# The dilated layer as one rolling sequence: four heads at a time, pair steps between the next heads' products

## The reference, cut to what matters

```
for g, (window, dil) in enumerate(DIL_PAIRS):
    qg, kg = rope(q[g]), rope(k[g])
    o_g, lse_g = banded attention of qg, kg, v[g], every dil-th token
wts = softmax(lse over the groups)
branch = sum of wts[g] * o_g
mem_out = memory_attention(qm, mk, mv)
y = concatenate(branch, mem_out) * silu(gate)
h = layer_norm(ALPHA * h + y @ w_out)
```

## Time and profile before

| | us |
|---|---|
| median of 3 runs | 1480.76 |
| lowest, highest | 1479.58, 1488.71 |
| the profiled execution | 1486.72 |
| its span | 1484.9 |
| busy TensorE, VectorE, ScalarE, GpSimd | 1354.7, 875.3, 655.5, 67.2 |
| the dilated layer's products, first to last | 327.5 to 695.7 |

### The profile page before, as it was taken

The page is one execution under the profiler, slowest core; times in us unless marked ns, Lnnn a source line. Parts: engine busy times, 40 slices in busy tenths (PEclk is TensorE's granted clock), DMA queues, the critical chain, the costliest instruction groups (busy, mean ns, idle before and its releaser), DMA issues. The chain is left out here.

```text
span 1484.9 us, 19718 instructions
## 1 busy us (share of the span) xinstructions
PE 1354.7 (91%) x7972; PEld 1167.0 (79%) x7972; DVE 875.3 (59%) x1455; ACT 655.5 (44%) x905; POOL 67.2 (5%) x48
## 2 busy tenths in 40 slices
PE   6998988989997899988999868999999878999997
PEld 6887885668886678876887857799988867799996
DVE  6546594667843387445535587565456587565454
ACT  4523425434344444552432537354443446344432
POOL 0000000000004400150000000000000000000000
PEclk9998998999999999998999889999999988999999
DMA  9405530145552045423304333355654332355661
GB/s 301 143 29 170 170 114 29 32 139 170 173 196 86 29 149 189 144 86 120 113 30 132 124 99 114 94 176 184 200 181 150 124 121 85 114 175 177 188 200 70
DMA packets 134240, 197.52 MB, mean 133 GB/s; under 512 B 4332, under 2 KB 77318, under 8 KB 134022
## 3 DMA queue, kind: packets, MB, share of 16 engines
q1 hardware_dynamic: 134022, 196.22, 40.7%
q0 software_dynamic: 128, 0.04, 0.0%
HBM read 195.20 MB, written 1.05 MB: 132 GB/s over the span
## 5 line engine op out<-in xcount | busy, mean ns | idle before, releaser
L1209 ACT ACTIVATE w_hi<-w_raw 128x2048 fp32r<-128x2048 f32 (+5 forms) x190 | 346.8, 1828 | 628.0 <-PE bank L432 595.9
L1554 DVE TENSOR_TENSOR w_lo<-w_raw,w_hi 128x2048 fp32r<-128x2048 f32 (+5 forms) x190 | 414.0, 2185 | 209.6 <-ACT w_hi L1209 200.2
L430 PE MATMUL bank<-h_hi,w_hi 128*128 128x256 f32 x976 | 281.9, 289 | 11.4 <-DVE w_lo L1554 7.9
L431 PE MATMUL bank<-h_lo,w_hi 128*128 128x256 f32 x976 | 279.3, 286 | 0.0
L432 PE MATMUL bank<-h_hi,w_lo 128*128 128x256 f32 x976 | 279.1, 286 | 0.0
L430 PE MATMUL bank<-w_hi,r_hi 128*128 128x512 f32 (+3 forms) x536 | 207.1, 386 | 9.7 <-DVE w_lo L1554 7.0
L431 PE MATMUL bank<-w_lo,r_hi 128*128 128x512 f32 (+3 forms) x536 | 205.3, 383 | 0.0
L432 PE MATMUL bank<-w_hi,r_lo 128*128 128x512 f32 (+3 forms) x536 | 205.3, 383 | 0.0
L430 PEld LDWEIGHTS bank<-h_hi,w_hi 128*128 128x128 f32 x976 | 190.4, 195 | 17.4 <-issue 11.3
L430 PE MATMUL bank<-w_hi,h_hi 128*128 128x512 f32 (+3 forms) x464 | 182.6, 394 | 17.9 <-DVE arena L1957 10.0
L431 PEld LDWEIGHTS bank<-h_lo,w_hi 128*128 128x128 f32 x976 | 190.3, 195 | 0.6
(11 more groups left out here) (225 smaller groups left out, 1420.1 us busy)
## 6 DMA issues: line engine op xcount, KB each, us to landing
w_raw<-in_mlp_w SPq DMA_DIRECT2D x64, 1024.0 KB, 5.5
w_raw<-in_w_in_c SPq DMA_DIRECT2D x42, 1024.0 KB, 5.2
w_raw<-in_w_out SPq DMA_DIRECT2D x24, 1024.0 KB, 5.1
w_raw<-in_w_in_a SPq DMA_DIRECT2D x12, 1024.0 KB, 6.1
w_raw<-in_w_in_b SPq DMA_DIRECT2D x12, 1024.0 KB, 5.1
w_raw<-in_w_in SPq DMA_DIRECT2D x8, 1024.0 KB, 5.4
w_raw<-in_w_out SPq DMA_DIRECT2D x8, 512.0 KB, 3.8
w_raw<-in_w_in SPq DMA_DIRECT2D x4, 780.0 KB, 4.6
```

Source lines behind the costliest of these rows:

```text
L430: nc.tensor.matmul(o, lhs[0], rhs[0], start=start, stop=False)
L431: nc.tensor.matmul(o, lhs[0], rhs[1], start=False, stop=False)
L1209: nc.scalar.activation(w_hi[:, u % SPLIT_SLOTS, 0:kts * n], w_raw[:, u % RAW_SLOTS, 0:kts * n], ACT.Copy).then_inc(w_rounded.sem, w_rounde ...
L1554: v.tensor_tensor(w_lo[:, s, 0:m], w_raw[:, u % RAW_SLOTS, 0:m], w_hi[:, s, 0:m].bitcast(F32), ALU.subtract)\
```

## The change

The two halves become one sequence. Keys and queries are projected for four heads at a time: a unit holds 256 columns of the queries and the same 256 of the keys (`half_chunk`), loaded by two transfers (`load_unit`), so one chunk (two units) gives both for one group and four heads. The sections are keys and queries 0, memory query, values of the first eight heads, keys and queries 1, four gates, keys and queries 2, values of the last eight heads, keys and queries 3, and a tail with the last gate, the output product and the last four pairs. `C_STEP` says before which unit a pair's scores stand: pairs 0 to 3 at the gates, 4 to 7 in section 2, 8 and 9 (memory) at the second values, 10 to 13 in section 3. Behind that unit come the transposes of the pair before and the values of the one before that. All projections go round banks 0, 1, 2 (`C_BANK`), turns and transposed probabilities share banks 3 and 6, and bank 7 takes all head outputs. Masked scores, exponentials and scaled probabilities of a pair stay in one place (`c_slot`). ScalarE does the scaling (`pair_scaled`); GpSimd has no such work any more.

```diff
+        C_SECTIONS = [("qk", 0), ("qm",), ("v", 0), ("qk", 1), ("gates",), ("qk", 2), ("v", 1), ("qk", 3)]
+        C_EARLY_GATES = (4, 0, 1, 2)
+        C_STEP = {("gates", n): n for n in range(4)}
+        C_STEP.update({("qk", 2, 1 + n): 4 + n for n in range(4)})
+        C_STEP.update({("v", 1, n): 8 + n for n in range(2)})
+        C_STEP.update({("qk", 3, n): 10 + n for n in range(4)})
+        C_TAIL = 14
+        C_OUT_BANK = 7
+        C_TURN_BANK = (3, 6)
+        C_BANK = {}
+        for section in C_SECTIONS:
+            for n in range({"qk": 3, "v": 3, "qm": 1, "gates": 4}[section[0]]):
+                for b in range(NB if section[0] in ("qk", "v") else 1):
+                    C_BANK[(*section, n, b)] = len(C_BANK) % 3
...
+        def c_slot(q, par):
+            return masked[:, par, :] if q % 2 == 0 else prob[:, 2 + par, :]
...
+                    def half_values(vh, i):
+                        g, kh = i // 2, i % 2
+                        banks = [C_BANK["v", vh, g, b] for b in range(NB)]
+                        if kh == 0:
+                            for b in range(NB):
+                                if banks[b] in left:
+                                    pe.wait_ge(*left[banks[b]])
+                                left[banks[b]] = values_read.after((L, "v", vh, g, b))
...
+                    def heads_after(*at):
+                        if at in C_STEP:
+                            q = C_STEP[at]
+                            if q >= 1:
+                                pair_turned(q - 1)
                             if q >= 2:
-                                pair_values(half, q - 2)
+                                pair_values(q - 2)
+                    def qk_section(c):
+                        for i in range(6):
+                            heads_before("qk", c, i)
+                            half_chunk(c, i)
+                            heads_after("qk", c, i)
+                            if i in (2, 4):
+                                turn(c, i // 2 - 1)
...
+                    feature_major((L, "gate", 3), 2, rows_of(w, 0, KT, 3 * DIL_W + 3 * 256, 256), hT, reader=gate_read)
+                    turn(3, 2)
+                    residual(L, 0)
...
+                    pair_scores(q)
+                    out_unit(L, li, 0, 8, 2)
+                    pair_turned(q - 1)
+                    pair_values(q - 2)
...
+                if len(source.shape) == 3:
+                    sp.dma_start(dst, source).then_inc(w_loaded[u % RAW_SLOTS], 16)
+                else:
+                    for part in range(2):
+                        sp.dma_start(dst[:, :, part * n // 2:(part + 1) * n // 2], source[:, :, part, :]).then_inc(w_loaded[u % RAW_SLOTS], 16)
...
-            def scale_rows(key, slot, n):
-
-                pool.wait_ge(row_recip.sem, row_recip.at(key))
...
-                                nc.scalar.activation(prob[:, sl, :], masked[:, par, :], ACT.Exp, scale=-1.0,
+                                nc.scalar.activation(pr, pr, ACT.Exp, scale=-1.0,
...
+                    def pair_scaled(q):
+                        for par in range(2):
+                            sl, pr = 2 * (q % 2) + par, c_slot(q, par)
+                            act.wait_ge(row_recip.sem, row_recip.at((L, q, par)))
...
+                                ins = nc.scalar.activation(pr, pr, ACT.Copy, scale=S_(52 + 2 * sl, 1))
+                            ins.then_inc(probs_scaled.sem, probs_scaled.next((L, q, par)))
...
+                            if i % 2:
+                                if (vh, i) == (1, 1):
+                                    act.wait_ge(product_done.sem, product_done.at((L, "ao", 1)))
                                 for b in range(NB):
+                                    round_weights((L, "v", vh, i // 2, b))
+                                    act.wait_ge(product_done.sem, product_done.at((L, "v", vh, i // 2, b)))
+                                    nc.scalar.activation(cv[:, b, i // 2, :], bank[C_BANK["v", vh, i // 2, b]][:, :], ACT.Copy)\
+                                        .then_inc(values_read.sem, values_read.next((L, "v", vh, i // 2, b)))
...
+                    def heads(*at):
+                        if at in C_STEP:
+                            q = C_STEP[at]
+                            pair_max(q)
+                            pair_recip(q)
+                            if q == 5:
+                                heads_out(0, (L, "ao", 0), "early")
+                            elif q == 9:
+                                heads_out(1, (L, "ao", 1), "early")
+                            elif q == 11:
+                                heads_out(4, (L, "mo"), "early")
+                    def qk_section(c):
+                        for i in range(6):
+                            heads("qk", c, i)
+                            if i % 2:
+                                rope(c, i // 2)
```

More of the change, by code:

```diff
@@ L233, in build @@
         gate_read = Steps("gate_read")
+        rope_read = Steps("rope_read")
+        values_read = Steps("values_read")
         row_recip = Steps("row_recip")
@@ L440, in rT @@
                 return r_hi[:, k, cols], r_lo[:, k, cols]
[L442 to L456, removed]
             def feature_major(key, b, source, act, reader=act_read, hidden=None):
@@ L1205, in round_unit @@
                 _, kts, n = units[u]
-                act.wait_ge(w_loaded[u % RAW_SLOTS], 16 * (u // RAW_SLOTS + 1))
+                act.wait_ge(w_loaded[u % RAW_SLOTS], 16 * sum(len(units[n][0].shape) - 2 for n in range(u % RAW_SLOTS, u + 1, RAW_SLOTS)))
                 if u >= SPLIT_SLOTS:
@@ new lines, in _ @@
+                    qk_section(0)
+                    evac((L, "qm"), flat2(c_qmT), bank[C_BANK["qm", 0, 0]][:, :], scale=0.125)
+                    turn(0, 2)
+                    v_section(0, None)
+                    qk_section(1)
+                    for n, u in enumerate(C_EARLY_GATES):
+                        heads("gates", n)
+                        gate_raw(u, C_BANK["gates", n, 0])
+                        if n == 0:
+                            turn(1, 2)
+                    act.wait_ge(gate_read.sem, gate_read.at((L, "gate", 2)))
@@ L1382, in _ @@
+                    nc.scalar.activation(flat2(gate[:, 6:8, :]), bank[2][:, :], ACT.Silu).then_inc(gate_read.sem, gate_read.next((L, "gate", 3)))
+                    turn(3, 2)
+                    for q in range(C_TAIL, C_TAIL + 5):
+                        if q < C_TAIL + 4:
+                            pair_exp(q, 2)
+                            pair_scaled(q)
+                        pair_turned(q - 1, 2 if q < C_TAIL + 3 else 1)
                 round_weights((L, "wo", 1, 0), SPLIT_SLOTS - 1)
@@ L1887, in _ @@
+                    for q in range(C_TAIL, C_TAIL + 4):
+                        pair_max(q)
+                        pair_recip(q)
+                        if q == C_TAIL + 1:
+                            heads_out(2, (L, "ao", 2), "early")
+                    dve.wait_ge(gate_read.sem, gate_read.at((L, "gate", 3)))
+                    gated(L, 3, (L, "ao", 3), bank[C_OUT_BANK][:, :])
                 for n in range(2):
```

438 lines of the change are left out of this document (224 added, 214 removed).

## The result

| | before | changed |
|---|---|---|
| median of the runs beside each other, us | 1483.9 (4 runs) | 1504.3 (4 runs) |
| their range, us | 1479.6 to 1488.7 | 1501.2 to 1507.1 |
| profiled span, us | 1484.9 | 1505.3 |
| dilated layer in it | 327.5 to 695.7: 368.2 | 330.8 to 716.75: 386.0 |

The ratio is 1.0136, 95% interval 1.0093 to 1.0179. The forecast was no change, and 1504 lies above the range's end of 1500. Of the 20.4 us between the two spans 17.8 are in the dilated layer. It begins 3.3 us later, behind code that is the same in both.

What follows compares the result with a forecast made beforehand. It took TensorE, 91% busy, as the bound, idle in the dilated layer's pair stretches; 37.7 us removed against 38.1 added gave +0.4, so 1487.1 for the profiled execution and 1481 us for the median, range 1463 to 1500.

Steps and rivals of the forecast that it cites:

- removed: Two pair stretches of the dilated layer: at most 37.7 us comes back if every pair step hides behind a product unit.
- values: idle: Values sections: TensorE waits for ScalarE's bank copies, four bare gaps of 2.66 plus 1.8 and 1.5; 13.9 us without clock.
- rotations: First two key sections: VectorE's weight split delays the rotation that frees a bank; 2.2 us, nothing where pair steps lie between.
- memory gating: idle: Last key section: gating of the memory heads stands before VectorE's rotation; TensorE waits 3.0 us, 4.7 with the clock.
- turns behind transposed probabilities: Shared banks 3 and 6: ScalarE rounds, waits for the values, copies; TensorE waits 1.0 at four places, 4.0 us.
- tail: idle: Tail: waits of 2.2 (last turn), 0.8 (scores), 0.75 (residual) and 1.0 (low part), 4.75 us; 6.5 with clock.
- clock: TensorE at its lower clock behind bare gaps: six falls of 1.7 us, 10.2 us of the forecast.
- added: Dilated layer: new waits from values, rotations, memory gating, turns and tail, clock included, sum to 38.1 us.
- the residual's 0.75: Tail: TensorE's wait for a residual on bank 3, put at 0.75 us.
- one values gap of 1.8: Values gap partly covered by pair work: two probability copies and the wait for the output product come first; 1.8 us.
- rival 3: Pair sections: the rotation queued behind VectorE's reciprocals becomes the bound, 19 us more, 1500 us; chance 0.11.
- Rival 4: Split loads come late in the twelve units without pairs: 53 us less some 10 of lead, 1524 us; chance 0.03.

Runs made afterwards that it cites:

- E9: E6 plus, on ScalarE, the last turned keys copied before the Silu of gate tile 3: 1455.8 us, ratio 0.9810 to the kernel before.
- E1: Changed kernel with ScalarE's rounding called before the wait for the values in the step for transposed probabilities: 1485.2 us, ratio 1.0000 to before.
- E3: Changed kernel with VectorE's gating of the memory heads at pair step 12, not 11, behind the rotation: 1500.7 us, ratio 1.0111 to before.
- E8: Kernel before the change with the probabilities scaled on ScalarE behind their pair's exponentials, not on GpSimd: 1485.4 us, ratio 0.9996.
- E12: Changed kernel with the scaling of probabilities back on GpSimd, all else as changed: 1504.2 us, ratio 1.0128 to before.
- E7: Kernel before the change with its 36 loads of 1 MB for the dilated layer's products each halved into two transfers: 1484.4 us, ratio 0.9987.
- E5: Changed kernel with E1, E3, values copies before rounding, and transposed probabilities behind the values copies in the second values section: 1465.0 us, ratio 0.9874 to before.
- E10: Kernel before the change with ScalarE copying transposed probabilities before rounding the next unit: 1481.8 us, ratio 0.9981.
- E6: E5 with the scaling of probabilities on GpSimd instead of ScalarE: 1460.6 us, ratio 0.9838 to the kernel before.

## Why the prediction was wrong, step by step

**Where the loss lies.** In E9 the layer runs at a clock of 1.00, and TensorE is busy for 334.8 us with the same 2024 matmuls. I take this as the layer's work at full rate (an estimate: the mean is rounded, and the layer begins at the lower level in every kernel, for about 3 us in E9 and before and 4.5 in the changed one, where 128x512 products take 0.63 us until 335). The kernel before then lost 368.2 - 334.8 = 33.4 us, 24.8 idle and 8.6 to the clock; the changed one 51.2, 38.1 idle and 13.1 to the clock. The prediction had 37.7 and 38.1.

| term | predicted | measured |
|---|---|---|
| removed | 37.7 | 33.4 |
| values: idle | 13.9 | 15.4 (2.59 four times, 3.52, 1.52) |
| rotations | 2.2 | 2.4 |
| memory gating: idle | 3.0 | 3.1 |
| **turns behind transposed probabilities** | **4.0** | **10.4** (2.59 four times) |
| tail: idle | 4.8 | 6.6 (1.79, 1.44, 2.49, 0.85) |
| clock | 10.2 | 13.1 |
| added | 38.1 | 51.0 |

**The step that failed** is "Turns behind transposed probabilities": "ScalarE rounds, waits for the values, copies; TensorE waits 1.0 at four places". The code's order is wait, round, copy, because the wait stands in the step's loop and the rounding inside the copy's helper. That made 1.0 into 2.59, and by the same order the residual's 0.75 into 2.49 and one values gap of 1.8 into 3.52: 6.4 + 1.7 + 1.7 = 9.8 of the 13 us that the additions were short. E1 shows it, since one line that restores the order I had assumed gives 0.83 on average, 0.70 and 1.72. The piece of ScalarE's order ahead of the prediction could not have told: it names the wait for the values and the rounding's own wait for a finished unit by the same semaphore, so the code was the place to look. My bounds for the term (0 to 7) rested on the same reading and did not hold 10.4.

**What hung on it: the clock.** I had six falls of 1.7 us, all behind gaps named bare, none behind these four. The changed kernel shows six slow spells, one of them twice as long as the rest: 13.1 us against my 10.2, of which some 0.8 came in with the layer's slow start (an estimate from its 4.5 us against 3). That the sizes are near is partly luck. Only three of my six places were among them (behind the gaps that end at 389.44, 584.88 and 662.73); the others lie behind a turn's gap (535.52), the 3.52 and the residual, for which I had priced none. E1 took 6.4 us of busy time away with 12.4 of idle. Whether a gap of 2.59 us is followed by the lower level could not be told from its length: those ending at 389.44, 535.52 and 584.88 were, those at 404.76, 418.52, 514.50, 554.95 and 630.71 were not, nor was the 3.12, while the 1.79 was.

**The removed part was 4.3 too large.** I priced the two pair stretches with units that follow on one another. Beside a pair step a unit takes 5.57 us from start to start in the changed kernel (525.31 to 530.88) against the 5.44 of the earlier trace rows; 0.13 at each of the fourteen steps that lie beside a unit would be 1.8 (an estimate from one step). Two units with a turn take 12.1 (350.68 to 362.79) where the prices give 11.8. Where the rest of the 4.3 lies is open.

**Where luck came in.** E1 meets the forecast of no change, but its additions are 32.3 us (25.7 idle and 6.7 to the clock) and not 38.1, and the removed part is 33.4 and not 37.7. Both sides of the sum were too large by some 5 us.

**What was right.** GpSimd idle; no idle time in the gate section; the first values gaps (2.66 said, 2.59 measured); 3.1 us behind the memory gating; the rotations never the bound elsewhere but for the 0.46, so rival 3 did not come about although its 1500 is near the time: it has the right sum by the wrong mechanism, and E3 shows the one place is worth 3.2. Of what I had named as signs, the four values gaps were there, but only two of the four had slow matmuls behind them. Scaling two tiles on ScalarE takes 1.32 us (1.2 said), and E8 and E12 show that it is covered. The halved loads landed in 4.5 us, by the changed kernel's page:

```profile
w_raw<-in_w_in_c SPq DMA_DIRECT2D x48, 512.0 KB, 4.5
w_raw<-in_w_in_c SPq DMA_DIRECT2D x18, 1024.0 KB, 5.0
```

Rival 4 is out by these rows and E7, and none of ScalarE's waits in the layer is for a load. The Trainium skill's advice of transfers of at least 1 MiB (DMA: Bandwidth & Descriptors, Measured) did not decide anything here, since a unit's two halves still land before they are needed.

The tail's first wait was 1.79 where the table load, the gate and the hand-over were put at 2.2. The Trainium skill's drain (ScalarE: Activation LUTs, What ACT_TABLE_LOAD costs) would have made it 3.6; the load starts 0.02 us after the rounding of 1.06 us that began at 658.42 has ended, and the gate's copy 1.29 us after the load, so this trace shows none.

**Open.** The price of scaling on ScalarE once the waits are mended: 0.7 and 1.2 us in the layer, 3.6 and 4.4 in medians of four runs each, nothing in the changed kernel. Which gap is followed by the lower clock, and why, was not settled either.

## What to carry to other kernels

In a queue that runs in order, write down for every helper call what it does first, second and third, its waits included: a wait and a 1.9 us operation in the other order were worth 19 us here. When a schedule is made denser with fewer banks, the short copies that free a bank must come ahead of everything long in their engine's queue, and a long operation belongs into the time in which that engine would wait anyway. A dense order whose waits are few and bare can be mended one by one, and the gains add (E5); where one engine's list sets the pace they partly come back (E10).

## What the runs showed of the hardware

- **The same code before the layer took 7 us more or less from one profile to another.** The layer began between 324.1 (E12) and 331.4 (E7), and the granted clock in the 120 us before differs. Windows 200 to 320 of the kernel before, the changed kernel and E1, in this order:

```profile
200.00:320.00 120.00, 112.75 (x575) 82.54 (x573) 72.10 (x140) 52.09 (x120) 0.00 (x0) 0.93 0.25 81
```

```profile
200.00:320.00 120.00, 113.87 (x571) 82.21 (x570) 69.39 (x132) 52.09 (x120) 0.00 (x0) 0.90 0.25 79
```

```profile
200.00:320.00 120.00, 111.33 (x589) 82.47 (x589) 75.23 (x150) 53.48 (x122) 0.00 (x0) 0.95 0.28 88
```

- For a change in one layer, the layer's own length in the trace is thus a sharper measure than the span, and its idle and busy time are sharper still.
- GpSimd's scaling in place, 128x512, took 1.75 us on average in the kernel before and 1.97 in E6; what else ran beside it differed, and the cause was not tested.
